# The opening of a two-layer diffusion trunk: waits for small constants, the place of the prompt's normalising, and the engine that copies x

## What is computed

```
def _trunk(x, cond, ...):
    for i in range(DEPTH):                               # DEPTH = 2
        mod = (silu(cond) @ ada_w[i] + ada_b[i])         # 6 x 1024 columns
        sh1, sc1, g1, sh2, sc2, g2 = split(mod, 6)
        h = _rms_norm(x, norm_mix[i]) * (1.0 + sc1) + sh1
        out = _even_mixer(h, ...) if i % 2 == 0 else _pool_mixer(h, ...)
        x = x + g1 * out
        h = _rms_norm(x, norm_mlp[i]) * (1.0 + sc2) + sh2
        x = x + g2 * (square(relu(h @ mlp_w1[i])) @ mlp_w2[i])
    return _rms_norm(x, final_norm), ...
```

## Time and profile before

| | |
|---|---|
| median of 3 runs | 2529.99 us (2527.24 to 2534.19) |
| the profiled execution | 2525.03 us |
| its span, first to last instruction | 2522.5 us |
| granted TensorE clock, mean | 0.99 of 2.4 GHz |
| TensorE busy | 2441.2 us, 97% of the span |
| VectorE, GpSimd, ScalarE busy | 1544.1, 1028.1, 792.5 us |
| first matmul of the input product | 63.25 us |

### The profile page before, as it was taken

The page is one execution under the profiler, slowest core; times in us unless marked ns, Lnnn a source line. Parts: engine busy times, 40 slices in busy tenths (PEclk is TensorE's granted clock), DMA queues, the critical chain, the costliest instruction groups (busy, mean ns, idle before and its releaser), DMA issues.

```text
span 2522.5 us, 39010 instructions
## 1 busy us (share of the span) xinstructions
PE 2441.2 (97%) x14100; PEld 2141.8 (85%) x14100; DVE 1544.1 (61%) x2527; ACT 792.5 (31%) x1244; POOL 1028.1 (41%) x552
## 2 busy tenths in 40 slices
PE   7999999978999999999999999899999999999998
PEld 3988899977888888888888888787888888888887
DVE  6635752265368767777767776577333336767764
ACT  3311122133152222232232231664333334423322
POOL 7125322153113343333333333025565657776740
PEclk9999999989999999999999999999999999999999
DMA  7424533276201212111212112022434346343322
GB/s 252 153 79 147 167 101 107 109 234 218 77 18 59 100 58 75 58 58 60 98 62 71 58 58 75 17 105 85 147 108 144 110 165 237 119 148 116 125 84 84
DMA packets 153348, 274.12 MB, mean 109 GB/s; under 512 B 7428, under 2 KB 105512, under 8 KB 152232
## 3 DMA queue, kind: packets, MB, share of 16 engines
q1 hardware_dynamic: 150288, 263.22, 30.6%
q10 hardware_dynamic: 2968, 9.63, 1.2%
HBM read 204.66 MB, written 63.96 MB: 106 GB/s over the span
## 4 chain that ended last, share of the span: by engine, by line
PE 85%; DVE 6%; issue 3%; ACT 2%; POOL 2%; DMA 1%; ACTq 0%; POOLq 0%; SPq 0%; DVEq 0%
PE bank L457 79%; PE bank L2250 1%; PE bank L2403 1%; DMA ada_st_in<-in_ada_w_dram 1%; PE bank L2315 1%; PE bank L2278 1%; DVE X L1716 0%; POOL qsF L1586 0%; DVE ada_acc_in L1708 0%; DVE h1L L1882 0%; DVE vtok L1762 0%; DVE G3L L2134 0%; DVE ada_acc_mlp L1708 0%; DVE xgm L1875 0%; POOL ringL L1574 0%
## 5 line engine op out<-in xcount | busy, mean ns | idle before, releaser
L1716 DVE SCALAR_TENSOR_TENSOR X<-bank,mod,X 128x512 f32<-128x512 f32 (+1 forms) x852 | 544.9, 685 | 262.2 <-PE bank L457 261.8
L1371 POOL TENSOR_TENSOR ringL<-stage,ringH 128x2048 fp32r<-128x2048 f32 x66 | 314.1, 4758 | 591.8 <-ACT ringH L831 563.3
L457 PE MATMUL bank<-hH,ringH 128*128 128x512 f32 (+1 forms) x1248 | 446.2, 358 | 0.2 <-DVE hL L1882 0.2
L457 PE MATMUL bank<-hL,ringH 128*128 128x512 f32 (+1 forms) x1248 | 442.0, 354 | 0.0
L457 PE MATMUL bank<-hH,ringL 128*128 128x512 f32 (+1 forms) x1248 | 441.8, 354 | 0.0
L457 PEld LDWEIGHTS bank<-hH,ringH 128*128 128x128 f32 x1248 | 236.3, 189 | 33.7 <-DVE hL L1882 1.0
L457 PEld LDWEIGHTS bank<-hH,ringL 128*128 128x128 f32 x1248 | 236.0, 189 | 33.0
L457 PEld LDWEIGHTS bank<-hL,ringH 128*128 128x128 f32 x1248 | 236.2, 189 | 32.2
L831 ACT ACTIVATE ringH<-stage 128x2048 fp32r<-128x2048 f32 x65 | 124.0, 1908 | 313.4 <-PE bank L457 311.9
L457 PE MATMUL bank<-ringH,hH 128*128 128x256 f32 x640 | 184.1, 288 | 5.4 <-DVE hL L1685 5.4
L457 PE MATMUL bank<-ringL,hH 128*128 128x256 f32 x640 | 181.9, 284 | 0.0
(11 more groups left out here) (377 smaller groups left out, 5748.9 us busy)
## 6 DMA issues: line engine op xcount, KB each, us to landing
stage<-in_mlp_w_dram SPq DMA_DIRECT2D x64, 1024.0 KB, 5.7
ada_st_mlp<-in_ada_w_dram SPq DMA_DIRECT2D x18, 1536.0 KB, 8.2
stage<-in_ev_w_in_dram SPq DMA_DIRECT2D x14, 1024.0 KB, 5.1
mid_spill<-midT SPq DMA_DIRECT2D x56, 256.0 KB, 2.2
ada_st_in<-in_ada_w_dram SPq DMA_DIRECT2D x8, 1536.0 KB, 8.9
mid_spill<-midB SPq DMA_DIRECT2D x48, 256.0 KB, 2.0
ada<-in_ada_w_dram SPq DMA_DIRECT2D x8, 1024.0 KB, 13.2
x_spill<-X SPq DMA_DIRECT2D x1, 5120.0 KB, 18.7
```

Source lines behind the costliest of these rows:

```text
L457: mm = nc.tensor.matmul(out, a, b, start=first and n == 0, stop=last and n == 2, skip_group_check=chained)
L1371: nc.gpsimd.tensor_tensor(ringL[slot][:, :], stage[:, :], ringH[slot][:, :].bitcast(F32), ALU.subtract).then_inc(w_lo, 1)
L1716: V.scalar_tensor_tensor(out=X[:, d, cols(t)], in0=src[:, 0:TB[t][1]], scalar=gate_ap, in1=X[:, d, cols(t)], op0=ALU.mult, op1=ALU.add).th ...
```

## The change

SP's wait for the constants behind the first load goes. The identity's constant gets its own semaphore (`csm_in`), and TensorE transposes x's first token block before the other constants, which then follow. ScalarE's Silu moves behind square 4, its decay tables (now with ScalarE's own negation) into the input product, before unit 5's first copy. ScalarE copies the blocks 1, 4, 7, 10 and 13 of x out of the banks, each right before it squares that block; whoever waits for a block asks `x_block_in`. On VectorE the odd d's multiplications of the prompt (token block 2) move from before the bias to between the first and the second token block's modulation. On TensorE the column sums stand after weights 0, 2 and 4, and the first two batches of four row transposes after weights 5 and 6.

```
@@ -54,6 +54,7 @@
 IN_CUM = [sum(IN_GROUPS[:i]) for i in range(N_IN + 1)]
 
 
+XT_ACT = range(1, 2 * DT, 3)
 ADA_BATCH = NMOD // NCH
 ADA_IN_UNITS = {0: 0, 3: 1, 4: 2, 5: 3, 6: 4, 7: 5, 8: 6, 9: 7}
 ADA_IN = ADA_BATCH * len(ADA_IN_UNITS)
@@ -385,9 +386,10 @@
         return nc.alloc_semaphore(name) if n is None else [nc.alloc_semaphore(f"{name}{i}") for i in range(n)]
 
 
-    const_in, x_loaded, ada0_in = sem("const_in"), sem("x_loaded", NTB), sem("ada0_in", 8)
+    xt_act = sem("xt_act")
+    csm_in, const_in, x_loaded, ada0_in = sem("csm_in"), sem("const_in"), sem("x_loaded", NTB), sem("ada0_in", 8)
     fill_ok, vec_mm, vec_ev, silu_ok = sem("fill_ok"), sem("vec_mm"), sem("vec_ev"), sem("silu_ok")
-    dec_exp, dec_neg, dec_tab = sem("dec_exp"), sem("dec_neg"), sem("dec_tab")
+    dec_tab = sem("dec_tab")
     xt_mm, xt_ev, x_spilled, ada0_mm, mod_ok, gain_ok = (sem("xt_mm"), sem("xt_ev"), sem("x_spilled"), sem("ada0_mm"),
                                                          sem("mod_ok"), sem("gain_ok"))
     xn_v, row_ok, row_mm = sem("xn_v"), sem("row_ok"), sem("row_mm")
@@ -446,6 +448,11 @@
     def cols(tb):
         t0, w, _ = TB[tb]
         return slice(t0, t0 + w)
+
+    def x_block_in(i):
+
+        own = sum(a <= i for a in XT_ACT)
+        return (xt_act, own) if i in XT_ACT else (xt_ev, i + 1 - own)
 
     def pair_pass(out, w_hi_ap, w_lo_ap, m_hi_ap, m_lo_ap, first, last, weights_moving=False, chained=False):
 
@@ -589,14 +596,13 @@
         for tb in range(NTB):
             n0, n1 = TB[tb][0] // P, (TB[tb][0] + TB[tb][1]) // P
             sp.dma_start(xtok[:, n0:n1, :], x_in[tb]).then_inc(x_loaded[tb], 16)
-            if tb == 0:
-                sp.wait_ge(const_in, 16 * 10)
         for i in range(8):
             sp.dma_start(ada0[i][:, :, :], ada_v[0][:, :, i * UC:(i + 1) * UC]).then_inc(ada0_in[i], 16)
         raw_static(0)
         raw_static(1)
 
-        sp.wait_ge(xt_ev, GRP)
+        sp.wait_ge(xt_ev, GRP - len(XT_ACT))
+        sp.wait_ge(xt_act, len(XT_ACT))
         sp.dma_start(x_dram, X[:, :, :]).then_inc(x_spilled, 16)
         for v in range(N_IN):
             is_u = IN_UNITS[v][0] == "u"
@@ -836,7 +842,10 @@
         def square(i):
             t, d = BY_BLOCK[i]
             w = TB[t][1]
-            act.wait_ge(xt_ev, i + 1)
+            if i in XT_ACT:
+                act.wait_ge(xt_mm, i + 1)
+                nc.scalar.activation(X[:, d, cols(t)], bank[i % 4][:, 0:w], ACT.Copy).then_inc(xt_act, 1)
+            act.wait_ge(*x_block_in(i))
             if d == 0:
                 dst = acc[:, cols(t)]
             else:
@@ -869,7 +878,7 @@
                 nc.scalar.activation(hH[:, d, cols(tb)], hs_b[i % 2][:, 0:TB[tb][1]], ACT.Copy).then_inc(h_hi, 1)
 
 
-        act.dma_start(csm[:, :], small_const).then_inc(const_in, 16)
+        act.dma_start(csm[:, :], small_const).then_inc(csm_in, 16)
         vecs = [(0, c_ctx.rearrange("(k p) -> k p", p=P)), (8, c[0].rearrange("(k p) -> k p", p=P)),
                 (16, norm_mix.rearrange("l (k p) -> (l k) p", p=P)), (32, norm_mlp.rearrange("l (k p) -> (l k) p", p=P)),
                 (48, final_norm.rearrange("(k p) -> k p", p=P)), (56, od_pool_scale[0].rearrange("(k p) -> k p", p=P)),
@@ -878,18 +887,30 @@
             act.dma_start(rows[r:r + v.shape[0], :], v).then_inc(const_in, 16)
         act.dma_start(ada_rows[0:2 * NMOD, :], ada_b.rearrange("l (k p) -> (l k) p", p=P)).then_inc(const_in, 16)
         act.dma_start(dec[:, :], ev_decay.rearrange("o a h -> o (a h)").to_broadcast([P, 8])).then_inc(const_in, 16)
-        act.wait_ge(const_in, 16 * 10)
-        nc.scalar.activation(dec[:, :], dec[:, :], ACT.Exp).then_inc(dec_exp, 1)
-        act.wait_ge(dec_neg, 1)
-        nc.scalar.activation(kd[:, 0:4], ned[:, 0:4], ACT.Exp, scale=csm[:, P:P + 1]).then_inc(dec_tab, 1)
-        nc.scalar.activation(kd[:, 4:8], ned[:, 4:8], ACT.Exp, scale=csm[:, P + 1:P + 2]).then_inc(dec_tab, 1)
-        nc.scalar.activation(cd[:, :], ned[:, :], ACT.Exp, scale=float(P)).then_inc(dec_tab, 1)
-        act.wait_ge(vec_ev, 1)
-        nc.scalar.activation(sc2[:, :, :].rearrange("p k c -> p c k"), vec[:, 0:16].rearrange("p (c k) -> p c k", c=2),
-                             ACT.Silu).then_inc(silu_ok, 1)
+
+        def decay_tables():
+
+            act.wait_ge(csm_in, 16)
+            act.wait_ge(const_in, 16 * 9)
+            nc.scalar.activation(dec[:, :], dec[:, :], ACT.Exp).then_inc(dec_tab, 1)
+            act.wait_ge(dec_tab, 1)
+            nc.scalar.activation(ned[:, :], dec[:, :], ACT.Copy, scale=-1.0).then_inc(dec_tab, 1)
+            act.wait_ge(dec_tab, 2)
+            nc.scalar.activation(kd[:, 0:4], ned[:, 0:4], ACT.Exp, scale=csm[:, P:P + 1]).then_inc(dec_tab, 1)
+            nc.scalar.activation(kd[:, 4:8], ned[:, 4:8], ACT.Exp, scale=csm[:, P + 1:P + 2]).then_inc(dec_tab, 1)
+            nc.scalar.activation(cd[:, :], ned[:, :], ACT.Exp, scale=float(P)).then_inc(dec_tab, 1)
+
+        def silu():
+
+            act.wait_ge(vec_ev, 1)
+            nc.scalar.activation(sc2[:, :, :].rearrange("p k c -> p c k"), vec[:, 0:16].rearrange("p (c k) -> p c k", c=2),
+                                 ACT.Silu).then_inc(silu_ok, 1)
+
         act.wait_ge(fill_ok, 2)
         for i in range(GRP):
             square(i)
+            if i == HD:
+                silu()
             if i == 2 * DT - 1:
                 rms(0)
         rms(1)
@@ -919,6 +940,8 @@
                     apply_hi(1)
                 if ui == 0 and g == 2:
                     apply_hi(2)
+                if ui == 5 and g == 0:
+                    decay_tables()
                 if ui == 10 and g == 1:
 
                     act.wait_ge(pos_in, 16)
@@ -1717,27 +1740,34 @@
                                    op0=ALU.mult, op1=ALU.add).then_inc(ev, 1)
 
         dve.wait_ge(fill_ok, 2)
-        dve.wait_ge(dec_exp, 1)
-        V.tensor_scalar(ned[:, :], dec[:, :], -1.0, None, ALU.mult).then_inc(dec_neg, 1)
-        dve.wait_ge(vec_mm, 1)
-        V.tensor_copy(vec[:, :], bank[5][:, 0:68]).then_inc(vec_ev, 1)
-        dve.wait_ge(vec_mm, 2)
-        V.tensor_copy(adab[:, :], bank[4][:, 0:2 * NMOD]).then_inc(vec_ev, 1)
         for i, (t, d) in enumerate(BY_BLOCK):
             dve.wait_ge(xt_mm, i + 1)
-            V.tensor_copy(X[:, d, cols(t)], bank[i % 4][:, 0:TB[t][1]]).then_inc(xt_ev, 1)
-        for tb in range(NTB):
-            rstd(tb)
+            if i not in XT_ACT:
+                V.tensor_copy(X[:, d, cols(t)], bank[i % 4][:, 0:TB[t][1]]).then_inc(xt_ev, 1)
+            if i == DT - 1:
+                dve.wait_ge(vec_mm, 1)
+                V.tensor_copy(vec[:, :], bank[5][:, 0:68]).then_inc(vec_ev, 1)
+                dve.wait_ge(vec_mm, 2)
+                V.tensor_copy(adab[:, :], bank[4][:, 0:2 * NMOD]).then_inc(vec_ev, 1)
+        def normal_half(tb):
+
             dve.wait_ge(rstd_ok, tb + 1)
             for d in range(1, DT, 2):
                 V.tensor_tensor(xnT[:, d, cols(tb)], X[:, d, cols(tb)], acc[:, cols(tb)], ALU.mult).then_inc(xn_v, 1)
-        dve.wait_ge(row_mm, 1)
+
+        for tb in range(2):
+            rstd(tb)
+            normal_half(tb)
+        rstd(2)
+        dve.wait_ge(row_mm, 4)
         dve.wait_ge(vec_ev, 2)
         mods(0, 0, 2 * DT, 0, 1, 1)
         gains(0)
         dve.wait_ge(gain_ok, 1)
-        for tb in range(NTB):
-            apply(tb)
+        apply(0)
+        normal_half(2)
+        apply(1)
+        apply(2)
         def ada_batch(b):
             ada_part(b, 0, 0, 1)
 
@@ -1800,7 +1830,7 @@
         gains(1)
 
 
-        dve.wait_ge(dec_tab, 3)
+        dve.wait_ge(dec_tab, 5)
         dve.wait_ge(state_in, 32)
         for j, st in enumerate(ADVANCE):
             for d in range(2):
@@ -2256,34 +2286,46 @@
             pe.wait_ge(sum_add, ADDS[(tb, DT - 1)] + 1)
             nc.tensor.matmul(TOTAL_BANK[tb][:, 0:TB[tb][1]], ones[:, :], acc[:, cols(tb)], start=True, stop=True).then_inc(sum_mm, 1)
 
-        pe.wait_ge(const_in, 16 * 10)
-        nc.tensor.transpose(bank[5][:, 0:68], rows[0:68, :], ident[0:68, 0:68]).then_inc(vec_mm, 1)
-        nc.tensor.transpose(bank[4][:, 0:2 * NMOD], ada_rows[0:2 * NMOD, :], ident[0:2 * NMOD, 0:2 * NMOD]).then_inc(vec_mm, 1)
+        pe.wait_ge(csm_in, 16)
         pe.wait_ge(fill_ok, 2)
         for tb in range(NTB):
             pe.wait_ge(x_loaded[tb], 16)
             n0 = TB[tb][0] // P
             for d in range(DT):
                 i = DT * tb + d
-                after(pe, xt_ev, i - 3)
+                if i > 3:
+                    pe.wait_ge(*x_block_in(i - 4))
                 for n in range(TB[tb][1] // P):
                     mm = nc.tensor.transpose(bank[i % 4][:, n * P:(n + 1) * P], xtok[:, n0 + n, d * P:(d + 1) * P], ident)
                 mm.then_inc(xt_mm, 1)
+            if tb == 0:
+                pe.wait_ge(const_in, 16 * 9)
+                nc.tensor.transpose(bank[5][:, 0:68], rows[0:68, :], ident[0:68, 0:68]).then_inc(vec_mm, 1)
```

(24 more changed lines are left out.)

## The result

Over 22 runs of each, taken side by side, the median went from 2529.01 to 2534.43 us: a ratio of 1.0024, with 95% interval 1.0016 to 1.0031. By that ratio the change costs 6.1 us (4.0 to 7.8); the two medians alone differ by 5.4. The forecast was +4.2 us, 2534.2, and a difference under the 0.3% that it took as the least that shows. The total came out close to that. With 22 runs of each, though, the 0.24% is clear of no change. The terms behind the total came out only in part.

A forecast was written before the change was run, and what follows sets the result against it. TensorE, busy 2441.2 of 2522.5 us, was taken as the bound, so only the start of its steady work counted. Terms 3.9 + 0.5 - 2.5 + 1.3 + 1.0 gave +4.2 us, 2534.2 on the median; range 2525.5 to 2541.0.

The forecast's parts named there:

- The load: Rest of x lands at 14.4 and 17.0 instead of 17.6 and 20.2 us, hidden behind GpSimd's additions.
- The start of the modulation: ScalarE's copies of x, held by GpSimd's additions, start the modulation's matmuls at 29.9 instead of 25.96: +3.9 us.
- Cost nothing, margin 0.1 us: Silu with its 1.28 us table load, behind square 4, does not delay the 5th addition.
- 0.7 for the last seven blocks: Part of the clock's upper bound: 0.7 us for x's last seven blocks before the modulation, on top of 2.5.
- The small transposes between the weights: Eight of 16 row transposes now stand between modulation weights on TensorE: +0.5 us, bounds 0 and 0.6.
- The prompt's normalising ahead of the modulation: VectorE no longer normalises the prompt before the modulation's addition: -2.5 us ahead of the first product.
- Behind the first product: Four prompt multiplications lengthen VectorE's line before GpSimd's split of unit 1's weights: +1.3 us, bounds 0 and 3.5.
- The clock: Gaps of about 3 us in x's transposes drop TensorE to 1.2 GHz: +1.0 us, bounds 0 and 2.5 plus 0.7.
- the rival of a clock that falls for it: Modulation's matmuls start at 1.2 GHz, since transposes do not hold the clock: +6.4 us, 2536.4; chance 0.15.
- The sum: All terms of the opening together: +4.2 us, 2534.2 us on the median, too small to show.
- Copies not held: ScalarE's copies of x do not wait on GpSimd; modulation starts at 21.0: -5.7 us, 2524.3; chance 0.10.
- Constants that starve: Constants on ScalarE's queue, slowed by SP's, land at about 13.7 or later, delaying Silu and additions; slower; chance 0.10.

The follow-up runs named there:

- copies_off: The changed kernel with VectorE copying all 24 blocks of x; ratio to the kernel before 1.0005 (0.9996 to 1.0014).
- table_early: The changed kernel with one small unused Silu ahead of the squares, so the table load comes earlier; ratio to the kernel before 1.0014 (1.0005 to 1.0024).
- prompt_back: The changed kernel with VectorE's multiplications of the prompt back before the modulation's bias; ratio to the kernel before 1.0018 (1.0008 to 1.0028).
- prompt_moved_alone: The kernel before with only VectorE's multiplications of the prompt moved between the first and second block's modulation; ratio 0.9998 (0.9989 to 1.0007).
- copies_early: table_early with ScalarE's last four copies of x one to six squares earlier in its program; ratio to the kernel before 0.9988 (0.9976 to 1.0000).
- load_alone: The kernel before without SP's wait for the constants, nothing else changed; ratio 1.0008 (0.9998 to 1.0018).
- three_parts: copies_off, table_early and prompt_back together in the changed kernel; ratio to the kernel before 0.9993 (0.9983 to 1.0002).
- additions_shared: copies_early and prompt_back together, with seven of GpSimd's additions of squares given to VectorE; ratio to the kernel before 0.9980 (0.9970 to 0.9989).

## Why the prediction was right, point by point

**The load: right.** The second and third load of x landed at 15.62 and 18.20 (forecast 14.4 and 17.0), before anything waited for them, and bought nothing, since what TensorE waited for at the second block was ScalarE's copy (17.41). copies_off, without that wait, takes up the second block at 15.67 and starts the modulation 2.0 us before the kernel before. The last weight came at 43.09 (forecast 41.2), and none was late.

**The start of the modulation: mechanism right, size wrong.** The forecast was +3.9 us with copy 13 ended at 26.9; measured were +6.5 and 28.59. That ScalarE's copies are held by GpSimd's additions was so, shown by taking the copies out (−8.5), by adding them alone (+5.6) and by moving them alone (−7.4). Three things were missed in the size:
- The step "Cost nothing, margin 0.1 us" counted the Silu's table load and not the first one. Before, a load at 5.26 lay under the landing of the constants, and Silu's stood ahead of the first square. Now the first function of ScalarE is square 0, and its load ran only once block 0 was there (11.64), so the first addition came at 14.79 instead of the 13.1 forecast. table_early prices it: 1.5 us at the start of the modulation, and its copy 13 ends at 27.05, near the 26.9 forecast. The Silu's own load (18.21) cost nothing, as forecast: the additions kept their pace.
- The last seven blocks were transposed at half clock and took 0.43 instead of 0.335 us each. From the end of copy 13 to the modulation it took 3.9 us instead of 3.0. This had been put into the clock's term, as the upper bound's "0.7 for the last seven blocks".
- Block 0 landed at 9.53, 0.2 us later than forecast.

**The small transposes between the weights: right in kind.** From the modulation's start to the end of the row transposes it took 32.74 us instead of 31.88: +0.9, forecast +0.5, and outside the bounds of 0 and 0.6. Each of the two batches between the weights takes 0.41 us; the forecast had put a share of 8/16 of 1.15 us, 0.58, on both together.

**The prompt's normalising ahead of the modulation: the number right, the cause not.** The row transposes end at 65.19 and VectorE adds at 65.23, instead of 2.6 us later as before: −2.6, forecast −2.5. The forecast put this down to the move. prompt_back shows that in the changed kernel the wait goes without it, because the modulation is late: its first product is at 67.90, against 67.81. In the kernel before the move does win something ahead of the first product, 1.9 us in prompt_moved_alone. In the changed kernel, then, the move is not worth 2.5 - 1.3 = 1.2 us but costs 1.2.

**Behind the first product: right.** From the first product to unit 1 it took 32.26 us instead of 31.02: +1.25, forecast +1.3. VectorE's four multiplications took 1.42 us (forecast 1.4), and GpSimd's split became what TensorE waits for, with a gap of 1.74 us (forecast 1.3).

**The clock: right as a risk, its place not forecast.** The forecast's +1.0 was given to no stage. Busy time by stretch of the changed kernel, third value from the end the granted clock:

```profile
21.60:25.00 3.40, 3.39 (x15) 2.99 (x16) 1.38 (x2) 2.62 (x5) 2.97 (x4) 0.50 1.10 348
25.00:28.40 3.40, 0.97 (x9) 0.73 (x7) 1.62 (x3) 1.83 (x4) 3.11 (x3) 1.00 1.10 348
28.40:31.80 3.40, 3.16 (x14) 2.85 (x14) 2.43 (x6) 1.54 (x4) 2.97 (x4) 0.50 1.10 348
32.40:36.00 3.60, 3.55 (x17) 1.31 (x17) 0.00 (x0) 1.24 (x1) 1.89 (x2) 1.00 1.10 348
```

After each stop of about 2.65 us the transposes went on at 1.2 GHz, and each time the stretch behind them was at 2.4 GHz again. The modulation began at full clock, so the rival of a clock that falls for it did not come, and the only cost seen ahead of unit 1 was the 0.9 us above. The rule of the Trainium skill's page "TensorE: Matmul & The Clock Gate", section "Part 4: PE-mode transpose", by which transposes do not bring the full clock, would have had the modulation start at 1.2 GHz; this trace disagrees, with 1.00 from 32.40 on behind transposes alone. In table_early, though, the modulation did begin at half clock, with a stop of 2.92 us ahead of the last transposes instead of 2.67.

**The sum.** Forecast 3.9 + 0.5 − 2.5 + 1.3 + 1.0 = +4.2. Measured by position: 6.5 (start, clock included) + 0.9 − 2.6 − 0.2 + 1.2 = +5.8, where the −0.2 is the modulated input: 2.6 us from VectorE's addition (65.23) to the first product, 2.8 before, since GpSimd no longer worked beside it. Timed: +6.1. The total came within 2 us because the two terms that were too small were partly covered by the clock's allowance, not because each was right.

**The rivals.** Copies not held: refuted by the change's own rows and by copies_early, which is what that rival would have looked like. Constants that starve: in the changed kernel they landed at about 12.8 against 13.7 forecast, far from the 19.2 from which it decides; load_alone shows where even this delay costs 2.2 us.

## What to carry to other kernels

An instruction given to an idle engine costs what stands ahead of it in that engine's program, not what the engine's busy share suggests: the same five copies cost 5.6 us behind squares that wait for GpSimd, and nothing a few squares earlier. Before moving work out of a wait, look whether that wait still exists once the other parts of the change are in, and whether the line that the work is moved into has slack. And where an opening is reordered, ask which instruction is now the first to use ScalarE's tables, and what it waits for.

## What the runs showed of the hardware that was not expected

**The profiled span scatters in code that is the same.** From unit 1 to the end TensorE's program is the same in all these kernels. The stretch behind unit 1's start took 2428.2 us in the kernel before, 2434.5 in the changed one and 2442.3 in load_alone, and between these ends in all twelve profiled executions. By the clock records TensorE spent 44.5, 62.2 and 76.0 us of it at 1.2 GHz. Over the twelve executions the stretch grows by 0.46 us for each us at 1.2 GHz, with a correlation of 0.92. Not all is the clock: a load of modulation weights that the chain waits for took 8.90 us before and 10.55 in the changed kernel.

```profile
169.35 8.90 DMA ada_st_in<-in_ada_w_dram
```

```profile
175.23 10.55 DMA ada_st_in<-in_ada_w_dram
```

Over the twelve it took 8.90 to 10.82. It was long in load_alone (10.82) and copies_early (10.60), short in copies_off (9.01) and prompt_back (9.17), so it follows no single part of the change. Of the 12.1 us between the two spans, then, 6.3 lie behind unit 1 and are such scatter, while the 5.8 us of the opening are close to the timed 6.1. Why the clock falls more often in one execution than in another, and why this load is longer in some, stays open.

**The first table load.** A load took 1.28 us in every row, with 0.02 us or less between its end and the next activation where that had nothing else to wait for. The Trainium skill, "ScalarE: Activation LUTs", section "What ACT_TABLE_LOAD costs", counts a drain of 1.38 us on top; no row here shows one (the Silu's load at 18.21 begins 0.01 us behind the square before it), and table_early gained 1.5 us by removing one load from the path. The load may stand behind a wait: in the changed kernel it ran after the wait for block 0, while the one of the kernel before ran at 5.26, ahead of the wait for the constants (9.66). What makes the difference was not tried.

**VectorE beside GpSimd.** The four multiplications of the prompt on VectorE take 1.42 us alone and 6.76 (prompt_back), 7.30 (three_parts) and 7.31 us (additions_shared) where GpSimd's split of weights runs beside them. Duration of one in ns, least, median and most, in three_parts:

```profile
L1756 DVE TENSOR_TENSOR xnT<-X,acc x4: 932/939/4719, 51.3 to 57.6; 128x256 f32<-128x256 f32 x4
```

One of the four is held for about as long as the split takes (4.72 us beside a split of 4.68, which it began 0.6 us ahead of; 4.16 in prompt_back, where it began 0.6 us behind the split's start). The other three take 0.94 us each beside GpSimd's own multiplications, instead of 0.42 alone. The prediction's upper bound of 0.9 us each, taken from the earlier trace rows, is that of these three; had one of them met the split, the bound would have been too low by half.
